# Gate and up products of a feed-forward tile: one after the other, or interleaved by row block

## The reference

```
h = rms_norm(x, g)
x = x + 0.5 * ((silu(h @ w_gate) * (h @ w_up)) @ w_down)      # the last stage: without 0.5
```

## Time and profile before

| | before |
|---|---|
| median of 3 runs (lowest to highest) | 1293.68 us (1293.61 to 1294.24) |
| the profiled execution, its span | 1294.04 us, 1292.1 us |
| granted TensorE clock, mean | 0.997 |
| busy: TensorE, DVE, ScalarE, GpSimd | 1270.6 (98%), 1000.7 (77%), 726.0 (56%), 141.4 us (11%) |
| longest waits of TensorE | 5.5 us at the start (a DMA), then 1.2, 1.2, 1.0 in the mixers |

### The profile page before, as it was taken

The page is one execution under the profiler, slowest core; times in us unless marked ns, Lnnn a source line. Parts: engine busy times, 40 slices in busy tenths (PEclk is TensorE's granted clock), DMA queues, the critical chain, the costliest instruction groups (busy, mean ns, idle before and its releaser), DMA issues.

```text
span 1292.1 us, 24458 instructions
## 1 busy us (share of the span) xinstructions
PE 1270.6 (98%) x8455; PEld 1133.5 (88%) x8455; DVE 1000.7 (77%) x1863; ACT 726.0 (56%) x1331; POOL 141.4 (11%) x229
## 2 busy tenths in 40 slices
PE   7999999999999999999999999999999999999997
PEld 6999999789999999999999889999998868888886
DVE  6977778968887789777786769877777676977774
ACT  5655556766555556555555556555556655655553
POOL 5000003202330000000002202000005410000000
PEclk9999999999999999999999999999999999999999
DMA  9966665638996547666659537766657412666650
GB/s 269 273 197 187 184 189 149 153 111 202 271 273 193 183 143 226 188 187 193 182 153 253 177 101 229 217 183 190 193 156 183 135 47 82 203 189 193 184 174 33
DMA packets 295612, 233.57 MB, mean 181 GB/s; under 512 B 13180, under 2 KB 270532, under 8 KB 295552
## 3 DMA queue, kind: packets, MB, share of 16 engines
q1 hardware_dynamic: 288432, 213.80, 56.3%
q0 software_dynamic: 6688, 18.60, 5.8%
q10 hardware_dynamic: 432, 0.36, 0.1%
HBM read 229.79 MB, written 7.55 MB: 184 GB/s over the span
## 4 chain that ended last, share of the span: by engine, by line
PE 93%; DVE 2%; ACT 1%; DMA 1%; issue 1%; SPq 1%; POOL 0%; POOLq 0%; ACTq 0%; DVEq 0%
PE gu L2044 44%; PE y L2056 17%; PE y L2136 4%; PE gu L2428 4%; PE y L2098 3%; PE gu L2252 2%; PE y L2079 2%; PE gu L2079 2%; PE gu L2011 2%; PE gu L2221 2%; PE y L2466 1%; DMA sb_w_raw<-in_ffn_w_up 1%; PE gu L2443 1%; PE y L2455 1%; PE gu L2283 1%; PE gu L2512 1%
## 5 line engine op out<-in xcount | busy, mean ns | idle before, releaser
L2044 PE MATMUL gu<-sb_act_t,sb_w_hi 128*128 128x512 f32 x1680 | 587.6, 394 | 0.0
L1364 DVE TENSOR_TENSOR sb_w_lo<-sb_w_raw,sb_w_hi 128x1024 fp32r<-128x1024 f32 (+1 forms) x405 | 496.9, 1230 | 83.8 <-ACT sb_w_hi L911 77.5
L911 ACT ACTIVATE sb_w_hi<-sb_w_raw 128x1024 fp32r<-128x1024 f32 (+1 forms) x405 | 423.0, 1049 | 35.2 <-DMA sb_w_raw<-in_ffn_w_up 8.6
L2044 PE MATMUL gu<-sb_act_t,sb_w_lo 128*128 128x256 f32 x1680 | 434.7, 279 | 0.0
L2044 PEld LDWEIGHTS gu<-sb_act_t,sb_w_hi 128*128 128x128 f32 x1680 | 307.3, 188 | 55.3
L2044 PEld LDWEIGHTS gu<-sb_act_t,sb_w_lo 128*128 128x128 f32 x1680 | 316.1, 188 | 15.0
L2056 PE MATMUL y<-sb_hid_t,sb_w_hi 128*128 128x256 f32 x1216 | 218.5, 280 | 0.8 <-DVE sb_w_lo L1364 0.8
L977 ACT ACTIVATE sb_work<-gu 128x256 f32<-128x256 f32 x220 | 83.8, 382 | 203.1 <-PE gu L2044 197.7
L2056 PEld LDWEIGHTS y<-sb_hid_t,sb_w_hi 128*128 128x128 f32 x1216 | 190.9, 188 | 4.5 <-issue 1.1
L2056 PE MATMUL y<-sb_hid_t,sb_w_lo 128*128 128x256 f32 x608 | 170.2, 280 | 0.0
L1497 DVE TENSOR_TENSOR sb_work<-gu,sb_work 128x256 f32<-128x256 f32 x220 | 92.5, 422 | 69.4 <-ACT sb_work L977 69.4
(11 more groups left out here) (357 smaller groups left out, 1644.1 us busy)
## 6 DMA issues: line engine op xcount, KB each, us to landing
sb_w_raw<-in_ffn_w_gate SPq DMA_DIRECT2D x88, 512.0 KB, 3.9
sb_w_raw<-in_ffn_w_up SPq DMA_DIRECT2D x88, 512.0 KB, 3.9
sb_w_raw<-in_ffn_w_down SPq DMA_DIRECT2D x88, 512.0 KB, 3.4
sb_w_raw<-in_odd_w_qkv SPq DMA_DIRECT2D x24, 512.0 KB, 5.6
sb_w_raw<-in_w_gate SPq DMA_DIRECT2D x22, 512.0 KB, 3.9
sb_w_raw<-in_w_up SPq DMA_DIRECT2D x22, 512.0 KB, 3.9
sb_w_raw<-in_w_down SPq DMA_DIRECT2D x22, 512.0 KB, 3.5
sb_w_raw<-in_even_w_in SPq DMA_DIRECT2D x12, 512.0 KB, 3.9
```

The lines of the kernel that those rows point to most:

```text
L911: nc.scalar.activation(w_hi[:, slot, 0:w], w_raw[:, slot, 0:w], ACT.Copy).then_inc(hi_done, 1)
L1364: nc.vector.tensor_tensor(w_lo[:, slot, 0:w], w_raw[:, slot, 0:w], w_hi[:, slot, 0:w].bitcast(F32), ALU.subtract).then_inc(lo_done, 1)
L2044: ins = nc.tensor.matmul(gu[:, b, w, 0:width], part[:, s, cols], act_t[:, k, 0:width], start=(k == 0 and i == 0), stop=(k == KT - 1 and i ...
```

## The change

Inside `gate_up` the loop over w (gate, up) moves from the outside to the inside. For each of the 8 row blocks the two 512-column products come first (gate, then up), then the two 256-column ones; in the last row block the other way round. The wait for the weights is one, for both blocks, ahead of the tile; so is the wait for the PSUM banks, for both sums of the tile two before. Both blocks are released by the tile's last two products. Nothing changes on the other engines.

```diff
             def gate_up(n, slot, tile, b, between=None):
 
-                for w in range(2):
-                    s = (slot + w) % RING
-                    pe.wait_ge(lo_done, n + w + 1)
-                    if not isinstance(tile, int) or tile >= 2:
-
-                        pe.wait_ge(gu_summed, tile * 2 + (w - 3))
-                    for k in range(KT):
-                        if between and (w, k) == (0, KT - 2):
-                            between()
-                        cols = slice(k * P, (k + 1) * P)
-                        parts = [(w_hi, 2 * SEQ), (w_lo, SEQ)]
-                        if k == KT - 1:
-                            parts.reverse()
-                        for i, (part, width) in enumerate(parts):
-                            ins = nc.tensor.matmul(gu[:, b, w, 0:width], part[:, s, cols], act_t[:, k, 0:width],
+                s = [(slot + w) % RING for w in range(2)]
+                pe.wait_ge(lo_done, n + 2)
+                if not isinstance(tile, int) or tile >= 2:
+
+                    pe.wait_ge(gu_summed, tile * 2 - 2)
+                for k in range(KT):
+                    if between and k == KT - 2:
+                        between()
+                    cols = slice(k * P, (k + 1) * P)
+                    parts = [(w_hi, 2 * SEQ), (w_lo, SEQ)]
+                    if k == KT - 1:
+                        parts.reverse()
+                    for i, (part, width) in enumerate(parts):
+                        for w in range(2):
+                            ins = nc.tensor.matmul(gu[:, b, w, 0:width], part[:, s[w], cols], act_t[:, k, 0:width],
                                                    start=(k == 0 and i == 0), stop=(k == KT - 1 and i == 1))
-                    ins.then_inc(block_used, 1)
+                            if k == KT - 1 and i == 1:
+                                ins.then_inc(block_used, 1)
```

## The result

| | before | after |
|---|---|---|
| median, same chip | 1293.64 us (1292.7 to 1294.24, 4 runs) | 1302.73 us (1302.3 to 1303.89, 4 runs) |
| span of the profiled execution | 1292.1 us | 1300.8 us |
| DVE busy | 1000.7 us | 986.2 us |

DVE does the same work in both: its 1863 records add up to 1065.4 us before and 1064.1 after. Busy time fell because more of the records now stand back to back, where they overlap.

The account below looks back on a forecast made before the run. The prediction took TensorE almost alone to bound the kernel. Its terms, 0 + 3.8 + 1.47 + 0.45 + 1.28 + 1.65, sum to 8.65 us, giving 1302.7 us for the profiled execution and 1302.3 for the median, range 1296.5 to 1307.0.

Parts of the forecast that it names:

- opening: Program's start, where loads are late: tile 3 waits for its up block's split and starts 1.65 us later.
- four stage ends: Ends with 256-column down products: TensorE waits 0.95 us each for the last tile's hidden low part, 3.8 us together.
- second tile, three stages: Second tile of stages behind a mixer: waits for its up block's low split, 0.15 us each, 0.45 us together.
- third tile, two stages: Third tile of a later stage: the prediction gave no wait and no size for it.
- stage behind a stage: Second tile of the stage directly following another: waits for its up block's split with DVE late, 1.28 us.
- last stage's end: End of the last stage, where 512-wide down products cover less: hidden block ready 1.47 us later.
- products: The 105 gate_up calls: regrouping equal widths changes TensorE's streaming by 0, with bounds of 3 us either way.
- DVE's lateness in the mixers: Three mixers: DVE 0.7 us late net, where it may meet an attention chain; 0 to 1 us, not counted.
- Rival 1: Doubled pairs stream slower by 2 to 4 ns each, on top of the edges: 3 to 6 us; chance 0.13.
- Rival 2: Edges (stage ends and opening) are covered after all and nothing moves by 2.6 us: 1294 to 1296; chance 0.07.
- Rival 3: Grouping changes how stationary-block loads hide, so pairs get faster and the kernel ends below 1293.7; chance 0.06.
- Rival 4: Steady middle tiles stall because the burst of halves and splits misses the ring: 1323 at 0.2 us a tile; chance 0.03.

Follow-up runs that it names:

- e5: Kernel before, with only the gate block's release moved to up's last but one product: 1300.69 us, ratio 1.0061.
- e1: Changed kernel with the old gate_up for the last tile of each of the five stages: 1296.7 us, ratio 1.0029.
- e6: Changed kernel with one weight split moved behind the hidden tile's parts at a stage's end, on ScalarE and DVE: 1304.17 us, ratio 1.0088.
- e8: Kernel before, products in the old order, but both waits ahead of the tile and both blocks released by the last two products: 1301.53 us, ratio 1.0061.
- e11: The changed kernel measured once more, unaltered, against the kernel before: 1302.4 us, ratio 1.0072.
- e2: Changed kernel with the new gate_up only in tiles 4 to 20 of each stage, the old one in tiles 1, 2, 3 and 21: 1293.7 us, ratio 1.0008.
- e7: Kernel before, in the first stage the first down block's high part made ahead of the first hidden tile's: 1292.98 us, ratio 1.0001.
- e4: Kernel before, products and releases as they were, with the waits for both weight blocks and both PSUM banks ahead of the tile: 1295.67 us, ratio 1.0025.
- e3: Changed kernel with products alternating in width (gate wide, gate narrow, up wide, up narrow), both waits still at the head: 1300.34 us, ratio 1.0058.
- e9: Kernel before, with gate and up interleaved in alternating widths in tiles 4 to 20 of each stage only: 1291.57 us, ratio 0.9991.
- e10: Kernel before, with alternating widths in tiles 4 to 20 and the first down block's high part ahead of the first hidden tile's: 1291.68 us, ratio 0.9986.

## Why the prediction was right, step by step

Measured values are the steps in the start-to-start comparison of the two traces, us.

| term | predicted | measured |
|---|---|---|
| start of the program | 0 | -0.29 |
| opening | 1.65 | 2.08 |
| four stage ends | 4 x 0.95 | 4 x 1.04 |
| second tile, three stages | 0.45 | 0.45 |
| third tile, two stages | none | 0.28 |
| stage behind a stage | 1.28 | 0.86 |
| last stage's end | 1.47 | 1.46 |
| products | 0 | 1.07 (the remainder) |
| clock in before's mixer | none | -1.37 |
| sum | 8.65 | 8.7 |

- **Stage ends: right.** The chain through the queued split was put at 5.14 us from the switch to the end of the hidden low part and took 5.11. What was left out is the restart, 0.34 us for two products instead of 0.23; that is the 0.09 by which each end exceeded its price. e5 shows the release as the cause, e1 the last tile as the place, e6 the split as part of the chain.
- **Last stage's end: right to 0.01.** TensorE waited there before, too, so no restart was added.
- **Second tiles: right. Third tiles: missed.** I had costed everything behind the second tile at 0. The copy of the 1/rms row comes 2.1 us later because gate's seventh row block now starts 4.2 us into the tile instead of 2.1; up's split follows it on DVE and just misses TensorE. In e8, where the row is spread at its old place, the same tiles lose 0.07 to 0.08 instead of 0.14, so the late row is only part of it.
- **Stage behind a stage: right in mechanism.** Two waits came, 0.39 for the column sums and 0.77 for the split, 1.16 against 1.28. Some 0.3 came back at the 1/rms row, the upper end of what I had left out. The column sums' wait I had folded into the split's.
- **Opening: right for the third tile, small by 0.14 behind it.** The third tile starts at 34.80, 1.65 later than the 33.15 of before. I had put both starts 0.16 too late (34.96 and 33.31), and the errors cancel. The next down product is 1.79 later, the restart again. The table's 2.08 counts from the start of the program, which was 0.29 earlier in after; the loads that set the splits did not come earlier for it. There is luck in the agreement: in e11, the same kernel, the product behind the third tile is 1.48 later than in before instead of 1.79, and in e2, whose opening is that of before, the first down product comes 0.7 earlier than in before. One pair of traces fixes this term to some tenths at best.
- **DVE's lateness in the mixers, put at 0 to 1 us and not counted,** cost 0.04 us or less in each: the lag behind the first end is 3.07 and ahead of the next stage 3.11.
- **The products: a term wrongly put at nothing.** I took 0 from two adjacent pairs in a trace with 0.01 us of resolution. The pairs cost 0.010 us a tile, 0.7 ns for each of 14 doubled pairs. The bounds of 3 us either way held it.
- **Rival 1** had the right sign at a fifth to a third of its size. **Rival 2** fell: none of the ends was covered. **Rival 3** fell: the pairs did not gain. **Rival 4** fell: no middle tile waits.
- **The sum agreed better than its terms.** Products, third tiles, opening and ends were underpriced by about 2.1 us together. The stage behind a stage gave 0.4 of it back, the start 0.3 and the clock dip in the profiled before 1.4. Without the dip the two traces are 10.1 us apart, and the medians of the larger comparison 9.3. The 21 executions of before in it differ in their mean granted clock: the six at 0.999 average 1292.67 us, the eleven at 0.997 1293.67. Against the former the changed kernel's 1302.4 stands 9.7 higher. So part of the good agreement of 8.65 with the measured 9.1 to 9.3 is luck.

## What to carry over

When two accumulations that fed a consumer one after the other are interleaved, both end together. Where the next work is long this is free; price it where the stage ends, by following the consumer's program in order from the new completion time, with every unrelated piece queued in it, and then look for what those late pieces delay one tile further on. Read streaming cost over many tiles (16 starts apart), not from one pair. Before trusting a difference of a microsecond between two traces, compare them start to start: one dip of the clock in one of them can hide it, as here in before, or pass for an effect of the edit, as in e6 and e7.

## What the runs showed of the hardware

- The order of widths changes the pace of the same 32 products and 24 behind them, without any wait: 8.404 us a tile with equal widths in pairs (after, e1, e2, e6), 8.394 to 8.396 with gate and then up (before, e4, e5, e7, e8), 8.380 to 8.382 alternating (e3, e9, e10). Counting neighbours of equal width in the code gives 17, 3 and 1 a tile, and the steps of 0.010 and 0.013 us are not in proportion, so the number of such neighbours alone does not explain it. The bank changes once a tile in the old order, with every product in pairs, and every second product in the alternating one. Why stays open.
- A wait costs TensorE some 0.1 us beyond its length: the first two 256-column products behind it take 0.34 us instead of 0.23.
- The granted clock fell to 0.50 for a little over 3 us in the middle of some executions and not of others: in the last mixer (before and e1, against after, e2, e7, e9, e10 and e11 with the same work around it), at 996.3 us in e8, at 491.5 in e6 and at 12.4 in e3. In before it cost 1.4 us, in e6 1.5. TensorE's longest wait just ahead was 0.55 us in before and 1.0 in e6. What decides it is not shown.
